# Spreading two kinds of modulation rows over partitions with TensorE in place of a trip through DRAM

## The chip, the cores and the metric

The kernel runs on one core of one Trainium2 chip. The metric is the device time of one launch in microseconds (us). Three runs of the kernel before were timed; a separate profiled execution gave the trace that is read here.

## What is computed

The reference is one step of a small hybrid backbone over 384 tokens (128 context tokens and 256 latent tokens, width 1024, all fp32), in two layers. Layer 0 mixes with a gated linear attention and a spatial gating, layer 1 with grouped-query attention. Each mixer is followed by an expert layer. What matters here:

```python
mod = silu(cond) @ w + b                    # 6 rows of 1024 for each layer and stream
h = rms_norm(x, norm_g) * (1 + scale) + shift
x = x + gate * mixer(h)                     # m[0], m[1], m[2]: shift, scale, gate of the mixer
h = rms_norm(x, norm2_g) * (1 + m[4]) + m[3]
x = x + m[5] * hier_moe(h)                  # m[5]: the gate rows of the expert layer
```

There are two streams (context and latent), so each of the six parts is a pair of rows. `hier_moe` picks two of 32 experts for each token; each expert has three matrices of 1024 x 256 floats. The rows are needed on all 128 partitions, because tokens lie on partitions and channels along them.

## The kernel before

**Weights.** All large weights pass through `ring`, six slots of 2 MB. The SP queue issues the loads in one fixed order, and before each it waits until the slot's last content is used up (`used_up`). A modulation part `(layer, part)` takes two chunks of `w_mod`, so two slots. TensorE multiplies them (`mod_products`), ScalarE copies the partial sums (`mod_part_copy`), TensorE adds them and the bias up to four rows of 512 (`mod_sum`: two halves by two streams), and ScalarE copies these four rows into the ring slot of the second chunk (`mod_row_copy`, which counts `rest_row_ready`). So the second slot stays taken until the four rows have left it. GpSimd (POOL) stores them to a DRAM tensor `mod_rows` (`store_rest`, counted in `rest_stored`), and later loads them back, read once for each of the 128 partitions (`load_rows`): a part is then 1 MB in SBUF, in `gate_rows` (GT) or `shift_scale` (GS).

**The chunks around the expert layers.** Ahead of expert layer 0 the last three parts in the ring are `norm_1` = (0, 5), the gate rows of expert layer 0, in slots 0 and 1; `router` = (1, 0), the shift rows of the attention layer's norm, in slots 2 and 3; `places` = (1, 1), its scale rows, in slots 4 and 5. Ahead of expert layer 1 the last part is `norm_3` = (1, 5), its gate rows, with its first chunk in slot 5 and its second in slot 0.

**Expert layer.** The 32 experts are taken in 16 pairs; each pair needs three loads of 2 MB (gate, up, down). Pair 0 uses slots 0 to 2, pair 1 slots 3 to 5, and so on in turn. SP issues them in the order of the slots:

```python
for u in range(2):
    for a in range(3):
        before_first(3 * u + a)
        load_experts(l, a, 2 * u, 3 * u + a)
```

so slot 0 of layer 1 waits for the last use of `norm_3`, and everything behind it in SP's order waits too. In the loop SP loads gate and up of pair q once the gate and up products of pair q-2 are done, and down of pair q once its down products are done.

**Routing and the first pairs.** The order on TensorE is: logits of three token blocks (L938), `norm_u` products and sum between them, counts (L953, L955), in layer 0 also the sum of `router` and the products of `places`, then `first_row` (L964, after `routing_sb` 3l+2), the table of all places (L968, after `routing_sb` 3l+3), in layer 0 the sum of `places`, and then the turn of the first gathered rows (L980) and pair 0 (L1008 gate and up, L1027 down). POOL gathers the token rows of a pair from `h_rows` in DRAM by an indirect DMA (L594); before the first two gathers it has stored `norm_u` (and in layer 0 `router`), and after them it stores `places` and loads the broadcast rows (L496). ScalarE copies the turned rows (L1336) and makes SiLU (L1342). VectorE works out the routing and adds the results of each pair (L1767).

Of the kernel before, what the change touches and what calls it, by code (L numbers as in the profile page):

```python
# [25 lines left out]
P = 128  # L26
D = 1024
KC = D // P
NB = 3
# [95 lines left out]
def mods(group):  # L125

    start = 0
    for name, chunks in MOD_GROUPS.items():
        if name == group:
            return range(start, start + len(chunks))  # L130
        start += len(chunks)
# [39 lines left out]
def scaled(i):  # L171

    return MODS[i][1] in (1, 4)


def fills_of(j):
# [9 lines left out]
def build(nc, d, outs):  # L186
# [3 lines left out]
    def S(name):  # L190
        if name not in sems:
            sems[name] = ctx.enter_context(nc.semaphore(name))
        return sems[name]
# [7 lines left out]
    with ctx:  # L201
# [196 lines left out]
        def used_up(eng, j):  # L398

            name, n = CHUNKS[j]  # L400
            if name == "mod" and (n < 2 * FRONT or n % 2 == 0):
                eng.wait_ge(S("mod_part_ps"), n + 1)
            elif name == "mod":
                eng.wait_ge(S("rest_stored"), 32 * (n // 2 - FRONT + 1))
            elif name == "even_in":
                eng.wait_ge(S(("qk_ps", "v_ps", "g_ps", "vg_ps", "u_ps")[n]), (4, 3, 3, 3, 4)[n])
            elif name == "even_out":
                eng.wait_ge(S("even_out_ps"), 2 * NB - 1 + n)
            elif name == "odd_in":
                eng.wait_ge(S("odd_in_ps"), (3, 6, 12)[n])  # L410
            else:
                eng.wait_ge(S("odd_out_ps"), 2 * NB - 1 + n)
# [74 lines left out]
        def _(pool):  # L487
# [3 lines left out]
            def load_rows(u, part, dst, sem):  # L491

                n = dst.shape[1]
                l = u // 2
                src = mod_rows[l, 3 * (u % 2) + part[0]:3 * (u % 2) + part[1]].rearrange("a s n -> (a s n)")
                pool.dma_start(dst, src.rearrange("(o n) -> o n", o=1).broadcast_to([P, n])).then_inc(S(sem), 16)  # L496
# [40 lines left out]
            def store_rest(group):  # L537
                for i in mods(group):
                    pool.wait_ge(S("rest_row_ready"), i - FRONT + 1)
                    _, rows, gains = rest_buffers(i)  # L540
                    if scaled(i):
                        pool.tensor_tensor(rows, rows, gains, ALU.mult).then_inc(S("gains_applied"), 1)
                        pool.wait_ge(S("gains_applied"), sum(scaled(k) for k in range(FRONT, i + 1)))
                    store_mod(i, rows, "rest_stored")
                    pool.wait_ge(S("rest_stored"), 32 * (i - FRONT + 1))

            store_rest("even")
            pool.wait_ge(S("activated"), 1)
# [17 lines left out]
            def experts(l):  # L566
                u = 2 * l + 1

                def M(name):
                    return S(f"moe{l}_{name}")  # L570

                if l == 0:
                    pool.wait_ge(S("o_ready"), NB)
                    pool.wait_ge(S("ob_ready"), NB)
                    pool.wait_ge(S("stored"), 16 * 4)
                for v in range(2):
                    pool.memset(XS[v], 0.0).then_inc(S("rows_cleared"), 1)
                pool.memset(oh_sum[:, NB, :], 0.0).then_inc(S("rows_cleared"), 1)
                store_rest(f"norm_{u}")
                if l == 0:  # L580
                    store_rest("router")

                def column(field, q):
                    return tab[:, field:field + 1, bass.ds(q, 1)]

                def one(v):
                    return v.rearrange("p (f o) -> p f o", o=1)

                def gather(q, v, static=False):
                    row = one(first_row[:, q:q + 1]) if static else column(0, q)  # L590
                    pool.tensor_copy(one(from_row[v][:, 0:1].bitcast(U32)), row).then_inc(M("row_looked_up"), 1)  # L591
                    pool.wait_ge(M("row_looked_up"), q + 1)
                    pool.sem_inc(S("pool_waited"), 1)
                    pool.indirect_dma_start(XS[v], None, h_rows[l], bass.IndirectOffsetOnAxis(ap=from_row[v][:, 0:1].bitcast(U32), axis=0),  # L594
                                            bounds_check=T - 1, oob_is_err=False).then_inc(M(f"gathered_{v}"), 16)

                def pair(q, v):
                    pool.wait_ge(M("x_ps"), q * 2 + 2)
                    pool.sem_inc(S("pool_waited"), 1)
                    gather(q + 2, v)  # L600

                pool.wait_ge(S("rows_cleared"), 3 * (l + 1))
                pool.wait_ge(S("h_stored"), 16 * NB * (l + 1))
                pool.wait_ge(S("table_ready"), 2 * l + 1)
                for q in range(2):
                    gather(q, q, static=True)
                if l == 0:
                    store_rest("places")
                load_rows(u, (2, 3), gt_t[:, :], "gate_in")
                if l == 0:  # L610
                    load_rows(2, (0, 2), gs_t[:, :], "rows_in")
                pool.wait_ge(S("table_ready"), 2 * l + 2)
                R = rounds_of(pool, l)
                with pool.Fori(0, R * (PAIRS // 2)) as i:
                    for v in range(2):
                        pair(i * 2 + v, v)
                for v in range(2):
                    pool.wait_ge(M(f"gathered_{v}"), R * 128 + 16)
                pool.sem_inc(S("pool_waited"), 1)
# [29 lines left out]
        def _(pe):  # L649
# [276 lines left out]
            def experts(l):  # L926
# [7 lines left out]
                def logits(b):  # L934
# [3 lines left out]
                        pe.matmul(to, HT[:, b, k, :], WR[:, k, :], start=(k == 0), stop=False)  # L938
                    return pe.matmul(to, ones[0:1, :], BR, start=False, stop=True)

                pe.wait_ge(S("x_updated"), 2 * NB * (u - 1) + 4)
                logits(0)
                turn_for_router(u, 1)
# [19 lines left out]
                for i in range(6):  # L963
                    mm = pe.matmul(psum[:, 5, 0:2], in_slot[:, i, :], in_first[:, i, :], start=(i == 0), stop=(i == 5))  # L964
                mm.then_inc(S("routing_ps"), 1)
                pe.wait_ge(S("routing_sb"), 3 * l + 3)
                for i in range(6):
                    mm = pe.matmul(psum[:, 7, 0:2 * PLACES], in_slot[:, i, :], in_pair[:, i], start=(i == 0), stop=(i == 5))  # L968
                mm.then_inc(S("routing_ps"), 1)
                if l == 0:  # L970
                    mod_sum(mods("places")[0])

                def turn_rows(q, v, first=False):

# [182 lines left out]
        def _(act):  # L1157
# [145 lines left out]
            def experts(l):  # L1303
# [20 lines left out]
                act.wait_ge(S("router_sub"), l + 1)  # L1324
                act.activation(g_tmp, g_tmp, ACT.Exp)
                act.activation(rival[:, :, 0:1], rival[:, :, 1:2], ACT.Exp).then_inc(S("router_exp"), 1)
                if l == 0:
                    mod_copies(mods("router"))
                    mod_copies(mods("places"))

                def x_copies(q, first=False):
                    for half in range(2):
# [86 lines left out]
        def _(dve):  # L1419
# [28 lines left out]
            def norm_apply(u, b):  # L1448

                root = rs[:, b:b + 1]  # L1450
                if u == 0:
                    dve.tensor_scalar(H[:, b, :], X[:, b, :], root, None, ALU.mult).then_inc(S("h_ready"), 2)
                    return
                dve.wait_ge(S("rows_in"), 16 * u)
                if u == 4:
                    dve.scalar_tensor_tensor(H[:, b, :], X[:, b, :], root, GS[:, 0, 0, :], ALU.mult, ALU.mult).then_inc(S("h_ready"), 1)
                    return
                s = min(b, 1)
                for n in range(2):
                    cols = slice(n * 512, (n + 1) * 512)  # L1460
                    link(dve.scalar_tensor_tensor(H[:, b, cols], X[:, b, cols], root, GS[:, 1, s, cols], ALU.mult, ALU.mult))
                    dve.tensor_tensor(H[:, b, cols], H[:, b, cols], GS[:, 0, s, cols], ALU.add).then_inc(S("h_ready"), 1)
# [5 lines left out]

            def update(u, ps, buf):

                dve.wait_ge(S("gate_in"), 16 * (u + 1))
                for c in range(6):
                    b, n = divmod(c, 2)
                    cols = slice(n * 512, (n + 1) * 512)
                    dve.wait_ge(S(ps), c + 1)
                    link(dve.tensor_tensor(buf[n], bank(OUT_BANKS[u][c]), GT[:, min(b, 1), cols], ALU.mult))
                    dve.tensor_tensor(X[:, b, cols], X[:, b, cols], buf[n], ALU.add).then_inc(S("x_updated"), 1)
                    if n == 1:
                        norm_block(u + 1, b)
                ht_low(u + 1, 2, ROUTER_TURN_BANK[u + 1] + 1)  # L1480
# [174 lines left out]
            def experts(l):  # L1655
# [166 lines left out]
                    for v in range(2):  # L1822
                        pair(i * 2 + v, v)
                dve.wait_ge(M("added"), R * (PAIRS * 6) - 6)
                dve.wait_ge(S("gate_in"), 16 * (u + 1))
                dve.wait_ge(M("x_sb"), R * (PAIRS * 2) + 2)

                def update_block(b):
# [100 lines left out]
```

## Time and profile before

| what | value |
|---|---|
| median of 3 runs | 1046.89 us (1042.3 to 1049.77) |
| profiled execution, its own time | 1044.07 us |
| its span in the trace | 1042.0 us |
| TensorE busy | 923.9 us (89%) |
| VectorE busy | 461.0 us (44%) |
| ScalarE busy | 226.1 us (22%) |
| GpSimd busy | 100.4 us (10%) |
| moved by DMA | 303.99 MB, mean 292 GB/s |
| mean granted TensorE clock | 0.953 |

The span runs from the first to the last instruction; some 2 us of the execution's own time lie around it. A busy share is an average over stages that have different limits, so what a change is worth has to be read in its stage.

### The profile page before, as it was taken

What the parts mean: (1) busy time and instruction counts of PE and PEld (TensorE: products, weight loads), DVE (VectorE), ACT (ScalarE), POOL (GpSimd) and SP (SyncE); (2) the same over time, 40 slices, a digit from 0 to 9 for tenths busy, and PEclk for the clock granted to TensorE, in tenths of its full rate; (3) what the DMA queues carried; (4) which work ended last, traced back from release to release, by engine and by line L of the source; (5) the groups of instructions that cost most, each with busy time, mean ns of one, the idle gap of its engine ahead of it and who ended that gap; (6) DMA issues with size and microseconds to landing.
All of it is one profiled execution on the core that took longest, in us unless ns stands there. A gap on an engine that the chain in (4) does not pass through costs nothing.

```text
span 1042.0 us, 11903 instructions
## 1 busy us (share of the span) xinstructions
PE 923.9 (89%) x4136; PEld 462.2 (44%) x4136; DVE 461.0 (44%) x1037; ACT 226.1 (22%) x458; POOL 100.4 (10%) x164
## 2 busy tenths in 40 slices
PE   2699999999799999999988997899589999999970
PEld 0355454645344444444433465445434444444430
DVE  1257632244323543543555474624515435435454
ACT  2223132212211112112122115212122121111121
POOL 2300011300210000000001000020100000000000
PEclk9899999998799999999998999999689999999995
DMA  9992350948899999999998523021699999999911
GB/s 301 361 351 81 132 184 18 363 167 303 341 398 419 421 420 420 419 422 420 407 372 299 178 81 131 0 87 41 259 418 419 421 420 420 421 420 420 401 50 60
DMA packets 76423, 303.99 MB, mean 292 GB/s; under 512 B 9784, under 2 KB 10096, under 8 KB 50920
## 3 DMA queue, kind: packets, MB, share of 16 engines
q1 hardware_dynamic: 66072, 277.08, 67.2%
q0 software_dynamic: 9040, 21.77, 5.9%
q10 hardware_dynamic: 1280, 4.72, 1.2%
q8 instruction: 20, 0.33, 0.1%
q14 instruction: 11, 0.09, 0.0%
HBM read 310.80 MB, written 5.32 MB: 303 GB/s over the span
## 4 chain that ended last, share of the span: by engine, by line
PE 70%; DMA 14%; DVE 7%; issue 3%; ACT 3%; SPq 2%; POOL 0%; POOLq 0%; DVEq 0%; ACTq 0%
PE psum L1008 18%; PE psum L692 16%; PE psum L1027 8%; DMA ring<-in_w_exp_up 7%; PE psum L764 4%; PE psum L890 4%; PE psum L716 3%; PE psum L980 3%; DVE ht L1767 3%; DMA arena<-h_rows,arena 3%; DMA ring<-in_w_in_odd 2%; DMA ring<-in_w_mod 2%; PE psum L938 1%; PE psum L1131 1%; PE psum L788 1%
## 5 line engine op out<-in xcount | busy, mean ns | idle before, releaser
L1008 PE MATMUL psum<-ring,arena 128*64 128x512 f32 x1024 | 229.6, 601 | 7.4 <-DMA ring<-in_w_exp_up 3.8
L692 PE MATMUL psum<-ring,ht 128*128 128x512 f32 (+1 forms) x432 | 171.9, 555 | 3.4 <-ACT ht L1199 2.7
L1008 PEld LDWEIGHTS psum<-ring,arena 128*64 128x64 f32 x1024 | 82.9, 139 | 151.3 <-issue 151.0
L1027 PE MATMUL psum<-ring,arena 128*64 128x512 f32 x512 | 116.9, 598 | 8.8 <-DVE ht L1767 7.1
L692 PEld LDWEIGHTS psum<-ring,ht 128*128 128x128 f32 x432 | 81.9, 192 | 86.2 <-issue 78.2
L1767 DVE TENSOR_TENSOR ht<-ht,psum 128x512 f32<-128x512 f32 x180 | 110.6, 681 | 4.1 <-PE psum L995 2.2
L1811 DVE TENSOR_TENSOR arena<-arena,psum 128x256 f32<-128x256 f32 x32 | 13.5, 421 | 186.0 <-ACT arena L1342 186.0
L1798 DVE SCALAR_TENSOR_TENSOR y_low<-psum,arena,y_top 128x512 fp32r<-128x512 f32 x64 | 48.0, 751 | 83.6 <-ACT y_top L1349 83.6
L1349 ACT ACTIVATE y_top<-psum,arena 128x512 fp32r<-128x512 f32 x64 | 44.0, 687 | 181.7 <-PE psum L1027 181.7
L994 PE MATMUL psum<-y_top,to_token 128*128 128x512 f32 x192 | 78.6, 409 | 3.5 <-DVE y_low L1798 3.5
L995 PE MATMUL psum<-y_low,to_token 128*128 128x512 f32 x192 | 75.6, 394 | 0.0
L716 PE MATMUL psum<-ring,cond_silu 128*32 128x512 f32 x384 | 48.0, 637 | 23.3 <-DMA ring<-in_w_mod 23.3
L1027 PEld LDWEIGHTS psum<-ring,arena 128*64 128x64 f32 x512 | 34.3, 136 | 76.6 <-issue 56.0
L1342 ACT ACTIVATE arena<-psum 128x256 f32<-128x256 f32 x32 | 12.3, 385 | 211.7 <-PE psum L1008 211.7
L980 PEld LDWEIGHTS psum<-ident,arena 128*128 128x128 f32 x272 | 34.1, 195 | 34.5 <-issue 32.1
L980 PE MATMUL psum<-ident,arena 128*128 128x128 f32 x272 | 41.0, 296 | 8.0 <-DMA arena<-h_rows,arena 8.0
L591 POOL CAST arena<-arena 128x1 uint32 (+1 forms) x36 | 7.1, 196 | 405.6 <-PE psum L980 391.2
L1336 ACT COPY arena<-psum 128x512 f32<-128x512 f32 x68 | 36.7, 589 | 31.4 <-PE psum L980 31.4
L764 PE MATMUL psum<-ht,ring 128*128 128x384 f32 x128 | 43.1, 493 | 0.0
L890 PE MATMUL psum<-ring,ht 128*128 128x512 f32 x96 | 41.9, 592 | 0.0
L994 PEld LDWEIGHTS psum<-y_top,to_token 128*128 128x128 f32 x192 | 36.2, 188 | 12.5 <-issue 5.3
L594 POOL DMA_INDIRECT arena<-h_rows,arena x36 | 37.2, 1033 | 31.2 <-POOL arena L591 30.0
(292 smaller groups left out, 869.4 us busy)
## 6 DMA issues: line engine op xcount, KB each, us to landing
ring<-in_w_exp_gate SPq DMA_DIRECT2D x32, 2048.0 KB, 18.0
ring<-in_w_exp_up SPq DMA_DIRECT2D x32, 2048.0 KB, 22.9
ring<-in_w_exp_down SPq DMA_DIRECT2D x32, 2048.0 KB, 20.5
ring<-in_w_mod SPq DMA_DIRECT2D x24, 2048.0 KB, 18.2
ring<-in_w_in_even SPq DMA_DIRECT2D x5, 2048.0 KB, 19.9
shift_scale<-mod_rows POOLq DMA_DIRECT2D x3, 2048.0 KB, 11.3
ring<-in_w_in_odd SPq DMA_DIRECT2D x3, 2048.0 KB, 21.2
ring<-in_w_out_even SPq DMA_DIRECT2D x2, 2048.0 KB, 8.5
```

The lines of the kernel that those rows point to most:

```text
L692: mm = pe.matmul(psum[:, to, 0:cols], HT[:, b, k, :], w[:, k, :], start=(k == 0), stop=(k == KC - 1))
L716: mm = pe.matmul(psum[32 * j:32 * j + 32, to, :], cond_silu[:, k, 2 - 2 * half:34 - 2 * half], w[:, k, :], start=(half == 0 and r == 0), s ...
L764: mm = pe.matmul(psum[:, to, 0:T], w[:, k, c * P:(c + 1) * P], HT[:, :, k, :], start=(k == 0), stop=(k == KC - 1))
L890: mm = pe.matmul(bank(OUT_BANKS[0][c]), HT[:, b, k, :], w[n][:, k, :], start=(k == 4), stop=(k == 3))
L980: t = pe.transpose(psum[:, half, kk * P:(kk + 1) * P], XS[v][:, 4 * half + kk:D:KC], ident[:, :])
L994: pe.matmul(to, to_token[v][:, b * P:(b + 1) * P], Y_HI[:, cols], start=True, stop=False)
L995: pe.matmul(to, to_token[v][:, b * P:(b + 1) * P], Y_LO[:, cols], start=False, stop=True).then_inc(M("back_ps"), 1)
L1008: mm = pe.matmul(psum[64 * e:64 * e + 64, 2, :], XT[:, k, 64 * e:64 * e + 64], RG[:, 3 * v:3 * v + 2, e, k, :], start=(k == 0), stop=(k == ...
L1027: mm = pe.matmul(psum[64 * e:64 * e + 64, 4 + n, :], HTS[v][:, k, 64 * e:64 * e + 64], RD[:, 3 * v + 2, e, k, n * 512:(n + 1) * 512], star ...
L1349: act.activation(Y_HI[:, n * 512:(n + 1) * 512], bank(4 + n), ACT.Copy, scale=token[v][:, 1:2]).then_inc(M("y_top"), 1)
L1767: dve.tensor_tensor(acc, acc, found, ALU.add).then_inc(M("added"), 1)
L1798: dve.scalar_tensor_tensor(Y_LO[:, cols], bank(4 + n), token[v][:, 1:2], Y_HI[:, cols], ALU.mult, ALU.subtract).then_inc(M("y_low"), 1)
```

## The change

Two parts of layer 0's tail, `norm_1` and `router`, and `norm_3` ahead of expert layer 1, no longer go through DRAM. TensorE multiplies the four rows by a one-hot matrix (one column of the identity's first four rows, repeated over 128 columns), which puts one of the four rows on all 128 partitions of a PSUM bank; four such products make a part. ScalarE copies each bank into GT or GS. Three banks are used in turn, so the fourth and later products wait for a copy. The ring slot is free once the four products are done (`spread_ps`), not once a store has landed. `places` keeps its path through DRAM. On TensorE the products stand between L964 and L968, and in layer 0 the sum of `places` is moved ahead of them.

```diff
+SPREAD = [mods(name)[0] for name in ("norm_1", "router", "norm_3")]
+SPREAD_BANKS = {0: (0, 1, 4), 1: (2, 3, 0)}
+
+def stores_until(i):
+    return 32 * sum(k not in SPREAD for k in range(FRONT, i + 1))
...
             elif name == "mod":
-                eng.wait_ge(S("rest_stored"), 32 * (n // 2 - FRONT + 1))
+                if n // 2 in SPREAD:
+                    eng.wait_ge(S("spread_ps"), 4 * SPREAD.index(n // 2) + 4)
+                else:
+                    eng.wait_ge(S("rest_stored"), stores_until(n // 2))
...
-                store_rest(f"norm_{u}")
-                if l == 0:
-                    store_rest("router")
...
-                load_rows(u, (2, 3), gt_t[:, :], "gate_in")
                 if l == 0:
-                    load_rows(2, (0, 2), gs_t[:, :], "rows_in")
+                    load_rows(2, (1, 2), gs_t[:, 2 * D:4 * D], "rows_in")
...
+                def spread(i, done):
+                    pe.wait_ge(S("rest_row_ready"), i - FRONT + 1)
+                    for c in range(4):
+                        if done + c >= 3:
+                            pe.wait_ge(S("rows_spread"), 8 * l + done + c - 2)
+                        pe.matmul(bank(SPREAD_BANKS[l][(done + c) % 3]), ident[0:4, c:c + 1].broadcast_to([4, P]), rest_buffers(i)[1],
+                                  start=True, stop=True).then_inc(S("spread_ps"), 1)
...
                 mm.then_inc(S("routing_ps"), 1)
+                if l == 0:
+                    mod_sum(mods("places")[0])
+                    spread(mods("norm_1")[0], 0)
+                    spread(mods("router")[0], 4)
+                else:
+                    spread(mods("norm_3")[0], 0)
                 pe.wait_ge(S("routing_sb"), 3 * l + 3)
                 for i in range(6):
                     mm = pe.matmul(psum[:, 7, 0:2 * PLACES], in_slot[:, i, :], in_pair[:, i], start=(i == 0), stop=(i == 5))
                 mm.then_inc(S("routing_ps"), 1)
-                if l == 0:
-                    mod_sum(mods("places")[0])
+                pe.wait_ge(S("rows_spread"), (8, 12)[l])
...
+                def spread_copies(rows, done):
+                    for c in range(4):
+                        half, s = divmod(c, 2)
+                        act.wait_ge(S("spread_ps"), 8 * l + done + c + 1)
+                        act.copy(rows[:, s, half * 512:(half + 1) * 512], bank(SPREAD_BANKS[l][(done + c) % 3])).then_inc(S("rows_spread"), 1)
+
                 if l == 0:
                     mod_copies(mods("router"))
                     mod_copies(mods("places"))
+                act.wait_ge(S("x_updated"), 2 * NB * u)
+                spread_copies(GT, 0)
+                if l == 0:
+                    act.wait_ge(S("h_ready"), 2 * NB * (u + 1))
+                    spread_copies(GS[:, 0], 4)
...
-                dve.wait_ge(S("gate_in"), 16 * (u + 1))
+                dve.wait_ge(S("rows_spread"), (8, 12)[l])
```

VectorE also waits for `rows_spread` ahead of the attention layer's norm, and the counts of `gate_in` follow the loads that are left.

## Rows read from the trace of the kernel before

**Rows 1.** The page's strip of 40 slices, its row of GB/s.

```profile
GB/s 301 361 351 81 132 184 18 363 167 303 341 398 419 421 420 420 419 422 420 407 372 299 178 81 131 0 87 41 259 418 419 421 420 420 421 420 420 401 50 60
```

**Rows 2.** The page's DMA issues: size of one, median us to landing.

```profile
ring<-in_w_exp_up SPq DMA_DIRECT2D x32, 2048.0 KB, 22.9
...
shift_scale<-mod_rows POOLq DMA_DIRECT2D x3, 2048.0 KB, 11.3
...
gate_rows<-mod_rows POOLq DMA_DIRECT2D x4, 1024.0 KB, 9.5
```

**Rows 3.** Windows of expert layer 0: clock, DMA share and GB/s stand last.

```profile
261.00:263.00 2.00, 2.00 (x20) 0.73 (x13) 0.00 (x0) 0.34 (x1) 0.00 (x0) 1.00 0.50 74
263.00:284.00 21.00, 14.98 (x77) 8.64 (x76) 9.20 (x39) 3.53 (x7) 5.90 (x9) 0.78 0.99 401
284.00:288.00 4.00, 3.60 (x10) 1.28 (x12) 0.00 (x0) 1.40 (x2) 1.12 (x2) 0.50 0.43 117
...
361.00:517.00 156.00, 151.04 (x706) 71.58 (x706) 68.77 (x150) 28.67 (x51) 11.94 (x20) 1.00 1.01 420
```

**Rows 4.** Windows of expert layer 1, same columns.

```profile
733.00:740.60 7.60, 4.99 (x15) 2.53 (x14) 4.65 (x29) 2.17 (x4) 1.04 (x2) 0.50 0.13 19
...
835.00:986.00 151.00, 145.62 (x681) 69.34 (x680) 65.31 (x145) 27.66 (x49) 11.29 (x20) 1.00 1.01 420
```

**Rows 5.** The chain that ended last: start us, us, what.

```profile
361.35 7.10 PE psum L1008 x32
...
369.19 23.01 DMA ring<-in_w_exp_up
392.54 7.09 PE psum L1008 x32
...
921.87 22.84 DMA ring<-in_w_exp_up
945.05 7.09 PE psum L1008 x32
...
991.24 6.87 PE psum L1008 x32
```

**Rows 6.** SP's queue in time order: when the first expert loads are issued.

```profile
261.17 0.37 SPq L425 DMA_DIRECT2D ring<-in_w_exp_up  x1
...
739.14 0.37 SPq L425 DMA_DIRECT2D ring<-in_w_exp_gate  x1
```

**Rows 7.** Timeline of routing and the first turn in layer 0.

```profile
268.36 1.50 PE L964 MATMUL psum<-arena 128*128 128x2 f32 x12
...
273.10 4.37 PE L968 MATMUL psum<-arena 128*128 128x200 f32 x12 [3.24 <-DVE arena L1744]
...
277.91 1.05 PE L733 MATMUL psum<-ring,pick 128*4 128x512 f32 x2
...
279.32 0.58 ACT L1184 COPY ring<-psum 4x512 f32<-4x512 f32 x1 [10.24 <-PE psum L734]
...
281.55 1.94 PE L980 MATMUL psum<-ident,arena 128*128 128x128 f32 x8 [2.27 <-DMA arena<-h_rows,arena]
...
284.40 8.98 PE L1008 MATMUL psum<-ring,arena 128*64 128x512 f32 x32 [0.91 <-ACT arena L1336]
```

**Rows 8.** Timeline of routing in layer 1.

```profile
733.72 1.87 PE L733 MATMUL psum<-ring,pick 128*4 128x512 f32 x2
...
743.26 2.72 PE L964 MATMUL psum<-arena 128*128 128x2 f32 x12 [3.10 <-DVE arena L1726]
...
749.22 3.88 PE L968 MATMUL psum<-arena 128*128 128x200 f32 x12 [3.24 <-DVE arena L1744]
```

**Rows 9.** Timeline of layer 1's first turn and pair 0.

```profile
757.21 1.94 PE L980 MATMUL psum<-ident,arena 128*128 128x128 f32 x8 [4.11 <-DMA arena<-h_rows,arena]
...
759.92 8.45 PE L1008 MATMUL psum<-ring,arena 128*64 128x512 f32 x32 [0.77 <-ACT arena L1336]
```

**Rows 10.** TensorE's waits from 361 to 517 us: total, times, longest.

```profile
PE psum L1008 <- DMA ring<-in_w_exp_up: 1.3, 4, 0.3
```

More of the change, by code:

```diff
@@ L544, in store_rest @@
                     store_mod(i, rows, "rest_stored")
-                    pool.wait_ge(S("rest_stored"), 32 * (i - FRONT + 1))
+                    pool.wait_ge(S("rest_stored"), stores_until(i))
             store_rest("even")
@@ L1454, in norm_apply @@
                 dve.wait_ge(S("rows_in"), 16 * u)
+                if u == 2:
+                    dve.wait_ge(S("rows_spread"), 8)
                 if u == 4:
@@ L1469, in update @@
             def update(u, ps, buf):
-                dve.wait_ge(S("gate_in"), 16 * (u + 1))
+                dve.wait_ge(S("gate_in"), 16 * (u // 2 + 1))
                 for c in range(6):
@@ L1824, in experts @@
                 dve.wait_ge(M("added"), R * (PAIRS * 6) - 6)
-                dve.wait_ge(S("gate_in"), 16 * (u + 1))
+                dve.wait_ge(S("rows_spread"), (8, 12)[l])
                 dve.wait_ge(M("x_sb"), R * (PAIRS * 2) + 2)
```

## The prediction

> **What bounds the kernel now.** I read the page's strip of slices first. It shows two long plateaus in which DMA moves 420 GB/s and is busy all the time [rows 1]: the two expert layers, in which nearly all bytes are expert weights. The second view, windows, makes it sharp: over 361 to 517 us and over 835 to 986 us the 16 DMA engines have a share of 1.01 and move 420 GB/s without a break [rows 3, 4]. TensorE is at 96 to 97% in the same windows, so it is not obvious which of the two sets the pace. The chain of waits tells: in layer 0 it passes through the load of an up matrix of 23.01 us just ahead of the gate and up products at 392.54 us, and in layer 1 through one of 22.84 us ahead of those at 945.05 us [rows 5]. TensorE's waits there look tiny, 1.3 us in all [rows 10]. That is how two nearly equal rates look: the bytes of a pair are 3 x 2.10 MB (2048 KB each, rows 2) and a gather, which takes at least 15.0 us at 420 GB/s, and the pairs come every (392.54 - 361.35) / 2 = 15.6 us. So what counts in an expert layer is when its stream of weights starts, what else is in that stream, and its rate. The end follows, as the wait at 945.05 us is only 46 us from the last pair's products at 991.24 us [rows 5].
>
> The third view is SP's queue. The second expert load of layer 0 is issued at 261.17 us, and the first of layer 1 at 739.14 us [rows 6]. In both cases SP was waiting for the store of a modulation part to land, `norm_1` and `norm_3`. Just before, DMA is nearly idle: 74 GB/s over 261 to 263 us, 19 GB/s over 733 to 740.6 us [rows 3, 4].
>
> **The change, part by part.**
>
> *Bytes removed.* In layer 0 the broadcast of the gate rows (1024 KB = 1.05 MB) goes, and of the broadcast into `shift_scale` (2048 KB) half goes; in layer 1 the gate rows go [rows 2]. All three were moved while DMA was the bound. At 420 GB/s each 1.05 MB is 2.5 us, so -5.0 us in layer 0 and -2.5 us in layer 1. The small stores (4 KB) are worth nothing in bytes. For memory transfers to SBUF the Trainium skill ("SBUF — State Buffer", its guidance on end-to-end transfer time) advises to reckon with about 358 GB/s, bound by HBM; the trace contradicts it here with 420 GB/s, and by the page's figure the three removals would come to 8.8 us, not 7.5, and the sum below would be some 1 us lower.
>
> *The release of slot 0 in layer 1.* Now this slot waits for the fourth product of the spread of `norm_3` (`spread_ps` 12), and these stand on TensorE behind L964. L964 waits for VectorE's routing until 743.26 us and takes 2.72 us, so it ends at 745.98 us [rows 8]. The trace has no product with four rows as input and 128 columns of weights; the nearest are L733 (128 rows, 4 columns, 512 moving): two in 1.87 us at half clock, that is 0.94 us each [rows 8], and two in 1.05 us at full clock, 0.52 us each [rows 7]. TensorE is at a granted clock of 0.50 in this stretch [rows 4], so I take 4 x 0.9 = 3.6 us with 2.1 us as the lower end. The fourth also waits for ScalarE's first copy. The trace's copies of 512 PSUM columns take 0.58 us [rows 7], and this one starts about 0.9 us after 745.98 us, so it is done before the third product is and costs nothing; ScalarE has nothing queued there, and if its first copy were late, each us of it would go onto the loads. So `spread_ps` 12 comes at 748.1 to 749.6 us, I take 749.3 us. SP issues the load then rather than at 739.14 us: 10.2 us later (9.0 to 10.6). Behind this load stand all six first loads in SP's order, as slot 0 is first.
>
> Of these 10.2 us the removed gate rows give 2.5 us back. The first gather (some 48 rows of 4 KB, 0.2 MB by 768 assignments over 16 pairs) now moves while DMA is idle: 0.5 us. Net: **+7.2 us** on every load of layer 1 (6.0 to 8.0).
>
> *Does it reach the end?* Pair 0 starts at 759.92 us now, because the turn of its rows waited 4.11 us for a gather that shared DMA with the weights [rows 9]. That wait goes: the gather is issued as before, on an idle DMA. L968 starts at 749.5 us in place of 749.22 us, as the spread fills TensorE's wait of 3.24 us [rows 8]. But what is late next is the weights: issued at 749.3 us, data from about 1.5 us later (SP issues at 739.14 us, and the window's idle part ends at 740.6 us, rows 4, 6), 4.2 MB for gate and up take 10 us, so pair 0 starts at 761.5 to 762.5 us, 2 us later. The later pairs follow the weights, as the plateau is the bound: they are 7 us later, and so is the end.
>
> *The releases in layer 0.* Slot 0 is free as before. Slot 1 now waits for `spread_ps` 4. On TensorE, L964 ends at 269.86 us; then the moved sum of `places`. It takes 1.9 us now, from the end of L968 at 277.47 us to the copy at 279.32 us, so it ends at about 271.9 us. Its inputs are there, and it is hidden in the wait for VectorE, which ends at 273.10 us. The products of `norm_1` follow. ScalarE first copies the two results of `places`, 0.58 us each [rows 7], so its first spread copy starts at 273.1 us and ends at 273.7 us; the fourth product waits for it and ends at 274.3 us. From there on the pace is ScalarE's copy, 0.55 us: the eighth product ends at 276.5 us (`spread_ps` 8, slot 3). L968 is queued behind the eighth product and starts at 276.5 us in place of 273.10 us; VectorE's table waits for it, as does the turn for pair 0. L968 then ends at 280.9 us at most, and the turn, which waited 2.27 us for its gather until 281.55 us [rows 7], is not later. Slot 1, issued at 274.4 us, has landed by 281 to 282 us, so pair 0 starts at about 284 us, as now (284.40 us, rows 7). POOL loses two stores in front of the first gathers and is a little earlier; nobody needs it.
>
> The weights of slots 1 and 2, issued at 261.17 us and behind it, move 13.2 us later, and slots 3 and 4 some 4 us later. In bytes: over 263 to 284 us DMA moved 401 GB/s and over 261 to 263 us 74 GB/s, 8.6 MB, plus 0.5 MB up to 288 us [rows 3]; the new stream starts at 276.0 us and moves 5.2 MB by 288.4 us, where the old one is back at the full rate. One gather of 0.25 MB goes into the idle stretch. So 9.1 - 5.4 = 3.7 MB are missing, 8.7 us; the two removed broadcasts give back 2.1 MB, 5.0 us. That leaves 3.7 us; with the second gather in the idle stretch too it would be 3.1 us. I take **+3.3 us** (1.5 to 4.5). The layer is bound by the stream from 392 us at the latest, so these 3.3 us reach its end, and the loads for the attention layer behind it.
>
> *The rest.* VectorE's waits for `rows_spread` are met hundreds of us before they are asked. 12 products and 12 copies are 6 to 11 us of TensorE and 7 us of ScalarE, in stretches in which both waited; their cover is VectorE's routing, and without it they would cost the 3 us by which the spread of layer 0 outlasts it.
>
> **Sum.** 7.2 + 3.3 = 10.5 us on the profiled execution's own 1044.07 us gives 1054.6 us. This execution lies 2.8 us under the median of 1046.89 us and inside the runs' spread, so the median after should lie between 1054.6 and 1057.4 us; I give 1055.
>
> **The rivals.**
>
> *The cushion absorbs it (not slower).* If TensorE and not DMA sets the pace of the pairs, a late start of the stream is caught up. The six slots let loads run ahead by two pairs, and TensorE's busy 96% and its waits of 1.3 us speak for it [rows 3, 10]. It decides if a pair takes TensorE 15.6 us even with weights at hand. Then layer 1 pays only pair 0's 2 us and layer 0 nothing: 1046 us. The unbroken 420 GB/s and the chain through 23 us loads speak against it. Chance 0.25 with the cases in which half is absorbed.
>
> *The bytes win (faster).* If the first products after L964 came early and pair 0 were not held, the removed 7.5 us would remain: about 1037 us. Against it stands SP's order, which puts the first load behind L964 in any case. Chance 0.04.
>
> *The start costs more.* TensorE idles in layer 1 from about 756 to 762 us and pair 0 then runs at half clock (8.45 us at a clock partly 0.5 now, 13 us at worst by twice 6.87 us, rows 5, 9); gate and up of pair 2 are issued late and the stream breaks for 2 to 4 us; or in layer 0 the copies and products run one after the other, 8 x 0.5 us more. 1058 to 1061 us. The queue holds six loads of 5 us each at that time, which speaks against a break. Chance 0.16.
>
> The forecast has 0.55. The range of 8 in 10 takes in its bounds (7.5 to 12.5 us), the spread of the runs and the near part of both neighbours: 1047 to 1062 us. About 1% (10.5 us) is what a measurement of this kernel can tell from no change. The forecast lies right at that border, so its chance is split almost evenly; with the rivals: faster 0.04, same 0.50, slower 0.46.
>
> **What the profile after would show.** The first expert load of layer 1 issued at 748 to 750 us plus layer 0's shift, behind four products of 0.5 to 0.9 us; DMA near zero from 733 us until then; pair 0's products released by DMA and not by ScalarE; L1008 of the last pair 10.5 us later than 991.24 us; DMA's share at 1.01 in both plateaus. In layer 0, a gap without traffic from 261 to 276 us. The forecast is wrong if the plateaus show DMA under 1.00 (TensorE is the bound), if pair 5 or so of a layer is no later than now, or if the loads leave within 5 us of their old place.

## The result, and the profile after

The kernel after took 1060.62 us in the median of four runs (1057.52 to 1063.9), the kernel before 1047.17 us. The ratio is 1.0134, with a 95% interval of 1.008 to 1.0189, so it is 1.3% slower. Six later runs of the same kernel gave 1.016 (1.013 to 1.0191). The profiled execution took 1057.87 us, its span is 1055.8 us, 13.8 us more than before.

The strip of slices of the page after, its row of GB/s, answers to [rows 1]. Both plateaus are there at 420 GB/s; what has changed most is ahead of them (slice 11 with 197 in place of 341, and slices 27 to 29 with 10, 60 and 123 in place of 87, 41 and 259).

```profile
GB/s 307 362 331 80 126 189 16 368 155 299 197 421 419 420 421 420 419 421 420 406 379 327 123 122 88 76 10 60 123 421 419 421 419 420 421 420 420 410 61 60
```

The windows of layer 0 and layer 1 after, with granted clock, DMA share and GB/s last, answer to [rows 3, 4]:

```profile
263.00:277.00 14.00, 14.00 (x68) 5.74 (x68) 7.13 (x29) 4.45 (x8) 3.61 (x5) 0.87 0.07 19
277.00:279.00 2.00, 2.00 (x4) 0.91 (x3) 0.00 (x0) 0.67 (x2) 1.71 (x3) 0.50 0.81 168
279.00:284.00 5.00, 5.00 (x7) 1.46 (x5) 0.00 (x0) 1.69 (x4) 0.06 (x1) 0.50 0.96 383
...
361.00:523.00 162.00, 156.98 (x730) 74.39 (x730) 73.43 (x158) 29.01 (x51) 12.93 (x21) 1.00 1.01 420
```

```profile
752.00:757.00 5.00, 5.00 (x7) 1.60 (x6) 1.39 (x6) 1.69 (x4) 2.90 (x3) 0.50 0.18 45
...
849.00:1000.00 151.00, 145.47 (x680) 73.41 (x679) 64.83 (x144) 27.64 (x49) 11.23 (x20) 1.00 1.01 420
```

Where DMA moved 401 GB/s over 263 to 284 us before, it now rests until 277 us. The plateaus have kept their rate and their share of 1.01.

The timeline of the kernel after, of layer 0 and then of layer 1, answers to [rows 6 to 9]. L981 is the `first_row` of before's L964, L955 the spread, L1354 its copy, L991 before's L968, L1030 before's L1008, and the L437 rows are SP's first loads.

```profile
268.59 1.50 PE L981 MATMUL psum<-arena 128*128 128x2 f32 x12
...
271.61 12.34 PE L955 MATMUL psum<-ring,ident 4*128 4x512 f32 x16
...
277.14 0.37 SPq L437 DMA_DIRECT2D ring<-in_w_exp_up  x1
```

```profile
746.94 2.72 PE L981 MATMUL psum<-arena 128*128 128x2 f32 x12 [3.10 <-DVE arena L1762]
...
749.59 7.19 PE L955 MATMUL psum<-ring,ident 4*128 4x512 f32 x8
...
755.11 0.58 ACT L1354 COPY gate_rows<-psum 128x512 f32<-128x512 f32 x1 [1.12 <-PE psum L955]
756.71 4.37 PE L991 MATMUL psum<-arena 128*128 128x200 f32 x12
756.81 0.37 SPq L437 DMA_DIRECT2D ring<-in_w_exp_gate  x1
...
770.18 5.22 PE L1030 MATMUL psum<-ring,arena 128*64 128x512 f32 x12 [7.99 <-DMA ring<-in_w_exp_up]
```

The reader is to see three things. SP's first load of layer 1 leaves less than 0.1 us after the four products end (756.81 and 749.59 + 7.19 us). The later copies wait 1.07 to 1.12 us each for a product, and not the products for the copies. And pair 0 is released by its weights after 8 us of waiting, where before the gathered rows were the last to come.

The end of the chain after, against [rows 5]:

```profile
757.22 12.87 DMA ring<-in_w_exp_up
770.18 9.51 PE psum L1030 x32
...
1005.67 6.87 PE psum L1030 x32
```

**Where the time went.** Runs of one kernel differ by some us in stretches that the change doesn't touch, so I compare spans between two points inside an expert layer: from the start of `first_row` (L964, and the line that holds it in each other kernel) to the start of the last pair's gate and up products. In layer 1 this is 991.24 - 743.26 = 247.98 us before [rows 5, 8] and 1005.67 - 746.94 = 258.73 us after, 10.7 us more. In layer 0 it is 516.63 - 268.36 = 248.27 us before (the chain of waits has the last pair at 516.63 us) and 523.03 - 268.59 = 254.44 us after, 6.2 us more. That makes 16.9 us. The stretch from layer 0's last pair to layer 1's `first_row` was 2.7 us shorter (226.63 and 223.91 us), which the change doesn't explain.

### The profile page after: what moved, and what is told of

Its sections match the earlier page's. It is cut to its first block, busy times and chain, and to the rows that moved or that the text cites. A ratio compares the mean times of both kernels' runs of the same rounds, so it can differ in the third digit from the quotient of the medians.

```text
span 1055.8 us, 11956 instructions
## 1 busy us (share of the span) xinstructions
PE 940.1 (89%) x4160; PEld 475.4 (45%) x4160; DVE 460.6 (44%) x1037; ACT 232.7 (22%) x470; POOL 96.6 (9%) x156
## 4 chain that ended last, share of the span: by engine, by line
PE 67%; DMA 18%; DVE 5%; issue 3%; ACT 3%; SPq 2%; DVEq 0%; POOL 0%; ACTq 0%
PE psum L1030 18%; PE psum L700 16%; DMA ring<-in_w_exp_up 15%; PE psum L1049 7%; PE psum L772 4%; PE psum L898 4%; PE psum L724 3%; DVE ht L1803 2%; PE psum L1002 2%; DMA ring<-in_w_in_odd 2%; DMA ring<-in_w_mod 2%; PE psum L955 2%; PE psum L946 1%; PE psum L1153 1%; PE psum L796 1%
## 5 line engine op out<-in xcount | busy, mean ns | idle before, releaser
L1030 PE MATMUL psum<-ring,arena 128*64 128x512 f32 x1024 | 229.7, 599 | 20.6 <-DMA ring<-in_w_exp_up 15.8
L1030 PEld LDWEIGHTS psum<-ring,arena 128*64 128x64 f32 x1024 | 90.3, 138 | 157.8 <-issue 148.9
L1049 PEld LDWEIGHTS psum<-ring,arena 128*64 128x64 f32 x512 | 34.3, 136 | 76.6 <-issue 56.0
```

Of the source, the lines that this page charges most:

```text
L1030: mm = pe.matmul(psum[64 * e:64 * e + 64, 2, :], XT[:, k, 64 * e:64 * e + 64], RG[:, 3 * v:3 * v + 2, e, k, :], start=(k == 0), stop=(k == ...
L1049: mm = pe.matmul(psum[64 * e:64 * e + 64, 4 + n, :], HTS[v][:, k, 64 * e:64 * e + 64], RD[:, 3 * v + 2, e, k, n * 512:(n + 1) * 512], star ...
```

## The experiments

All times of stretches below are between the same two points, in us:

| kernel | layer 0 | layer 1 | ratio to before (95%) |
|---|---|---|---|
| before | 248.27 | 247.98 | |
| after | 254.44 | 258.73 | 1.0134 (1.008 to 1.0189) |
| layer 1 undone | 254.85 | 247.87 | 1.0061 (1.0014 to 1.0107) |
| after, slots released at the sum | 245.37 | 242.65 | 0.988 (0.9842 to 0.9917) |
| before, late first load in layer 1 | 249.10 | 254.73 | 1.0064 (1.0034 to 1.0093) |
| before, without gate bytes in layer 1 | 249.47 | 245.41 | 0.9979 (0.9945 to 1.0013) |
| after, norm_3 products in fp32r | 254.81 | 254.60 | 1.0095 (1.0064 to 1.0125) |
| after, products of 128 rows | 252.96 | 258.12 | 1.0111 (1.0077 to 1.0145) |
| slots released, shift spread moved back | 242.54 | 242.78 | 0.9854 (0.9826 to 0.9881) |
| before, slots released at the sum | 246.16 | 244.94 | 0.9922 (0.9894 to 0.9949) |
| after once more | 253.19 | 258.45 | 1.016 (1.013 to 1.0191) |

Layer 0 was the same code in three of these kernels (before, late first load, without gate bytes) and gave 248.27 to 249.47; after's layer 0 stood in four (after twice, layer 1 undone, norm_3 in fp32r) and gave 253.19 to 254.85. So layer 0 owes 5.4 us by the means (248.9 and 254.3), known to about 1 us. Layer 1 repeats within 0.3 us and owes 10.7 us.

**Undo the change in layer 1 alone.**

```diff
-SPREAD = [mods(name)[0] for name in ("norm_1", "router", "norm_3")]
+SPREAD = [mods(name)[0] for name in ("norm_1", "router")]
...
+                if l == 1:
+                    store_rest("norm_3")
...
+                else:
+                    load_rows(3, (2, 3), gt_t[:, :], "gate_in")
...
-                else:
-                    spread(mods("norm_3")[0], 0)
```

> Kernel after, with the gate rows of expert layer 1 (norm_3) sent through DRAM again and layer 0 left as changed. Theory (the weight stream's start and bytes decide): in the two traces the last pair of layer 1 is 14.4 us late, and L964 of layer 1 was 3.7 us late already, so layer 1 owes 10.7 us; this kernel should lie 10 to 11 us under the kernel after and 3 to 4 us over the kernel before, with the first load of layer 1 issued 4.1 us before its L964, as before the change. Rival (the extra products and copies of TensorE and ScalarE cost the time, wherever they stand): 4 of 12 products go, so a third, some 5 us under the kernel after.

Measured: 1052.77 us, ratio 1.0061. In the timeline the first load leaves 4.1 us before `first_row`, as in the kernel before:

```profile
749.88 0.37 SPq L437 DMA_DIRECT2D ring<-in_w_exp_gate  x1
...
754.01 2.72 PE L985 MATMUL psum<-arena 128*128 128x2 f32 x12 [3.10 <-DVE arena L1765]
```

Layer 1 is back at 247.87 us. By the ratios the run is 0.7% (8 us) under the first runs of the kernel after and 1.0% (10 us) under the later ones, where I expected 10 to 11 us. It is 6 us over the kernel before, not 3 to 4: I had taken layer 0's share from how late layer 1's `first_row` was, and that includes the stretch between the layers, which varies. The stretches give layer 0's share as 5 to 6 us, which fits. This run alone doesn't tell work from waiting, as it takes both away.

**Release the slots at the sum, keep all products in place.**

```diff
+            if i in SPREAD:
+                rows = (HID_ROWS, HTS_ROWS, HID_ROWS)[SPREAD.index(i)]
+                return RC[:, slot, 0, :], rows, None
...
-                    eng.wait_ge(S("spread_ps"), 4 * SPREAD.index(n // 2) + 4)
+                    eng.wait_ge(S("mod_sum_ps"), n // 2 - FRONT + 1)
```

> Kernel after, with the four rows of the three spread parts written not into the ring but into the hidden-layer buffers that are free at that time, and SP released at the sum (mod_sum_ps). All products and copies stay where they are, so TensorE's work is the same. Theory: layer 1's first load leaves some 10 us before L964 ends (3 us earlier than in the kernel before), the stream is ahead and pair 0 starts as TensorE allows, near its place before; 1040 to 1050 us, so 10 us or more under the kernel after. Rival (TensorE's extra work is the cost): no change from the kernel after, 1058 to 1062 us.

Measured: 1034.35 us, ratio 0.988, so 26 us under the kernel after with the same products and copies, and under the expected 1040 to 1050 us.

```profile
734.47 0.37 SPq L442 DMA_DIRECT2D ring<-in_w_exp_gate  x1
...
741.60 2.72 PE L986 MATMUL psum<-arena 128*128 128x2 f32 x12 [3.10 <-DVE arena L1767]
744.25 7.19 PE L960 MATMUL psum<-arena,ident 4*128 4x512 f32 x8
...
758.19 7.09 PE L1035 MATMUL psum<-ring,arena 128*64 128x512 f32 x32 [0.81 <-ACT arena L1375]
```

The four products still take 7.19 us in front of pair 0, and pair 0 starts 16.6 us after `first_row`, as before the change (759.92 - 743.26 us, rows 8, 9). So this place costs TensorE nothing in layer 1. What cost the time was that SP waited for it. It was more than I expected; the last kernels below divide it. The rival, that the extra work is the cost, is out for the kernel after. In layer 0 the work isn't free once the slots are released early: pair 0 starts 20.9 us after `first_row` there, where it was 16.0 us before the change, and the kernel with the shift spread moved back shows what that is worth.

**The kernel before with a late first load and nothing else.**

```diff
+            sp.wait_ge(S("routing_ps"), 7)
             experts(1, lambda slot: used_up(sp, last_in(slot, len(CHUNKS))))
```

> Kernel before, with one wait more: SP issues the loads of expert layer 1 only after L964 of that layer (routing_ps 7). Nothing else is changed. Theory: the loads leave 7 us later (746 us in place of 739), everything in layer 1 after them too, so the run is 6 to 7 us longer. Rival (the six slots are a cushion, TensorE is the bound): 0 to 2 us longer, as pair 0 alone waits.

Measured: 1052.29 us, ratio 1.0064.

```profile
748.27 2.72 PE L965 MATMUL psum<-arena 128*128 128x2 f32 x12 [3.10 <-DVE arena L1727]
...
751.03 0.37 SPq L425 DMA_DIRECT2D ring<-in_w_exp_gate  x1
...
1003.00 6.87 PE psum L1009 x32
```

The first load leaves 2.76 us after `first_row` and not 4.12 us before it: 6.9 us later. The last pair is 6.75 us later (254.73 against 247.98). Within the scatter of 0.3 us all of the delay reaches the end; the six slots absorb none of it.

**The kernel before without 1 MB.** This kernel leaves out the broadcast of the gate rows in layer 1, so that layer 1's expert update uses other gate rows.

```diff
-                load_rows(u, (2, 3), gt_t[:, :], "gate_in")
                 if l == 0:
+                    load_rows(u, (2, 3), gt_t[:, :], "gate_in")
```

> Kernel before, which leaves out the 1 MB broadcast of the gate rows in expert layer 1 (the update at the end then multiplies by the attention layer's gate rows, so the output isn't the reference's). Theory: DMA is the bound, 1.05 MB at 420 GB/s are 2.5 us: 2 to 3 us shorter. Rival (TensorE is the bound): no change.

Measured: ratio 0.9979, with an interval that holds 1, so the runs alone show nothing. In the trace layer 1 is 2.6 us shorter (986.72 - 741.31 = 245.41 us), as 1.05 MB at 420 GB/s should be, against a scatter of 0.3 us.

**Cheaper products for norm_3.** The gate rows of layer 1 are rounded in this kernel from fp32 to fp32r, the type in which the kernel already keeps `y_top` and `y_low`.

```diff
+                        one_hot, rows = (pick_bias[0:4, 2 * c:2 * c + 1], ROWS_3) if l else (ident[0:4, c:c + 1], rest_buffers(i)[1])
-                        pe.matmul(bank(...), ident[0:4, c:c + 1].broadcast_to([4, P]), rest_buffers(i)[1], ...
+                        pe.matmul(bank(...), one_hot.broadcast_to([4, P]), rows, ...
```

> Kernel after; the rows and the one-hot of norm_3 are in fp32r, so that a product is one record and not two (the gate rows of layer 1 are rounded by it). Theory (the four products stand in front of SP's first load, each us of them goes onto the end): a product falls from 1.71 us to 0.6 to 0.9 us, the first load of layer 1 leaves 3 to 4.4 us earlier after the end of L964's products, and the last pair follows by as much, so 3 to 4.5 us under the kernel after. Rival (the products fill a wait of TensorE and cost nothing): no change from the kernel after.

Measured: 1058.12 us, ratio 1.0095. The timeline has four records where there were eight:

```profile
755.52 2.72 PE L985 MATMUL psum<-arena 128*128 128x2 f32 x12 [3.10 <-DVE arena L1766]
...
760.51 0.37 SPq L440 DMA_DIRECT2D ring<-in_w_exp_gate  x1
```

```profile
758.17 2.31 PE L959 MATMUL psum<-rows,pick_bias 4*128 4x512 f32 x4
```

The first load leaves 4.99 us after the start of `first_row`, where it was 9.87 us: 4.9 us earlier. Layer 1 is 4.1 us shorter, against a scatter of 0.3 us. So the price of the products is on the path, though not quite one for one. The runs alone don't separate this kernel from the first runs of the kernel after (1.0064 to 1.0125 against 1.008 to 1.0189); the stretch does.

**Products of 128 rows.**

```diff
-                        pe.matmul(bank(...), ident[0:4, c:c + 1].broadcast_to([4, P]), rest_buffers(i)[1],
+                        pe.matmul(bank(...), ident[:, c:c + 1].broadcast_to([P, P]), RC[:, slot_of(CHUNKS.index(("mod", 2 * i + 1))), 1, :],
```

> Kernel after; the one-hot has all 128 rows and so has the moving operand (the rows below the fourth are multiplied by zero), for all 12 products. It asks whether the half clock under the products, 1.71 us each, comes with their four rows. If so, the granted clock stays at or returns to 1.00 in layer 0's stretch, a product takes 1.0 us there, slot 1 and slot 3 are released 2 and 5 us earlier, and the run is 2 to 6 us shorter than the kernel after. If the clock falls for another reason (a share of idle time before them), the products stay at 1.7 us and the time stays.

Measured: 1060.43 us, ratio 1.0111, so not told apart from the kernel after. What it says of the clock stands in the last section. A product in layer 0 fell from 1.5 us (12.34 / 8) to 0.89 us (7.13 / 8):

```profile
274.99 7.13 PE L955 MATMUL psum<-ring,ident 128*128 128x512 f32 x16
...
278.72 0.37 SPq L437 DMA_DIRECT2D ring<-in_w_exp_up  x1
```

The first release (slot 1) came 6.8 us after `first_row` and not 8.6 us, 1.8 us earlier, and layer 0 is 1.5 us shorter than in the first trace of after, which is little more than the scatter of 1 us there. The release of slot 3 came 5.2 us earlier and added nothing that can be seen; the loads of slots 1 and 2, 2 MB each, had 10 us of transfer in front of it. In layer 1 the four products fell from 7.19 to 6.12 us, the first load left 1.1 us earlier, and the layer is 0.6 us shorter. I had expected 2 to 6 us in all; the stretches give 2.1 us. It is the start of the stream that counts, and not the release behind it.

**Release early, and move the shift rows' spread behind the expert layer.**

```diff
                 if l == 0:
                     mod_sum(mods("places")[0])
                     spread(mods("norm_1")[0], 0)
-                    spread(mods("router")[0], 4)
...
+                if l == 0:
+                    spread_shift()
                 combine(R * PAIRS - 1, 1)
```

> As the kernel with slots released at the sum, with the rows kept in free columns of the arena and the four products and copies of router (the shift rows of the attention layer) moved behind the loop of expert layer 0, where TensorE then waits for odd_in. Theory (with the slots released early TensorE sets layer 0's pace, as all its gate and up products start 15.1 us apart): the four products no longer stand ahead of pair 0, which starts some 5 us earlier after L964, and layer 0 is 4 to 5 us shorter; behind the loop they are hidden by the load of odd_in. 1028 to 1032 us. Rival (the stream is the bound after all, or the four products are on the path behind the loop): 1033 to 1037 us, as with the slots alone.

Measured: 1033.74 us, ratio 0.9854, in the range of the rival (1033 to 1037 us) and not in that of the theory. Pair 0 starts 15.4 us after `first_row` and not 20.9 us, 5.5 us earlier, but the last pair of layer 0 is only 2.8 us earlier. The chain of waits shows why: the gate and up products have 6.87 us and a distance of 15.1 us up to the pair at 422.45 us, and from the one at 468.15 us on 7.09 us and 15.4 us. I read this as TensorE setting the pace first, and then the stream. So each of the two theories holds for a part of the layer. Against the kernel with the slots alone (0.988, 0.9842 to 0.9917) the runs can't tell it apart; against the kernel before it is 1.5% faster (0.9826 to 0.9881), the lowest ratio here.

```profile
422.45 6.87 PE psum L1041 x32
...
468.15 7.09 PE psum L1041 x32
...
514.34 6.87 PE psum L1041 x32
```

**The kernel before with the slots released early.** All rows go through DRAM as before; only their source is outside the ring.

```diff
+            if i in OUTSIDE:
+                return RC[:, slot, 0, :], (ROWS_A, ROWS_B, ROWS_A)[OUTSIDE.index(i)], None
...
+                if n // 2 in OUTSIDE:
+                    eng.wait_ge(S("mod_sum_ps"), n // 2 - FRONT + 1)
```

> Kernel before (all rows through DRAM), with the four rows of norm_1, router and norm_3 kept in free columns of the arena and SP released at the sum. It asks what of the gain over the kernel before belongs to the early release and what to the removed broadcasts. If the start of the stream alone decides, layer 1 is 3 us shorter (first load 3 us earlier against L964, the 1 MB broadcast stays), layer 0 1 to 2 us shorter, in all 1042 to 1044 us. If the removed bytes are worth nothing, it is as fast as the kernel with the shift spread moved back, 0.985 of the kernel before.

Measured: 1038.42 us, ratio 0.9922 (0.9894 to 0.9949). That is between the two cases: under the 1042 to 1044 us of the start alone, and over 0.985.

```profile
731.12 0.37 SPq L434 DMA_DIRECT2D ring<-in_w_exp_gate  x1
...
738.25 2.72 PE L973 MATMUL psum<-arena 128*128 128x2 f32 x12 [3.10 <-DVE arena L1735]
```

The first load leaves 7.1 us before `first_row` and not 4.1 us, and layer 1 is 3.0 us shorter (244.94). Layer 0 is 2 to 3 us shorter than in the three kernels with before's layer 0. The two stretches together give 5 to 6 us and the runs 8 us; the rest isn't explained. So about half of the gain of the best version is the early release alone, and the other half comes with the spread in TensorE, once it no longer holds the slots: in layer 1 that is 2.2 us (244.94 and 242.78), near the 2.5 us of the removed gate rows, and in layer 0 3.6 us (246.16 and 242.54).

**The kernel after again.**

> The kernel after once more, on the chip of the run before it, for its distance to the kernel before and for the spread of the stretch between the two expert layers, which differed by 2.7 us between the first two traces. The sum of the two expert layers, taken from first_row to the last pair in each, should again be 16 to 18 us longer than before.

Measured: 1063.87 us, ratio 1.016 (1.013 to 1.0191). Against the stretches of the first trace before, the two layers are 4.9 and 10.5 us longer, 15.4 us in all, a little less than I expected. The first load of layer 1 leaves 9.87 us after `first_row`, as in the first trace. The stretch between the layers is 227.85 us here and was 223.91 us in the first trace of the same kernel, so that difference belongs to the run and not to the change. In the kernels with before's layer 0 it is 224.85 to 228.27 us.

## Why the prediction was right, and where it was too small

The direction, the place and the mechanism held: SP's first loads wait for the spread, and the stream of weights carries the delay to the end. The size was too small. The time of 1060.6 us lies near the upper end of the range of 1047 to 1062 us, above the stated 1055 us and above the 1054.6 to 1057.4 us of the sum. Of the three cases it was *slower by over 1%*, which I gave 0.46, less than the 0.50 for the case within 1%. That the range held is in part luck: it had been widened toward the rival *the start costs more*, in whose band of 1058 to 1061 us the time lies, and that rival had the wrong reason.

*The bound.* Right. Both plateaus keep 420 GB/s, and the late first load shows that 6.9 us of a later start are 6.75 us at the end. The cushion (0.25) is refuted for layer 1 as it was before. It exists in another state: in the kernel with the shift spread moved back, where the stream starts early, TensorE sets the pace for some ten pairs, and then the lead of the stream is used up. The prediction named a DMA share under 1.00 as the sign that TensorE is the bound. That sign doesn't work: in that kernel the share is 1.01 and the rate 420 GB/s over 361 to 452 us too. The distance of the pairs tells, 15.1 us there and 15.6 us in the kernel before.

*Bytes removed.* Right in layer 1: 2.6 us for 1.05 MB, where I had 2.5 us. For layer 0 no run takes its two broadcasts away alone; they are shown only together with the rest.

*The release of slot 0 in layer 1.* This is the step that failed in size. I took a product of the spread as 0.9 us, from L733 with "x2" and 1.87 us, which I read as two products [rows 8]. But `mod_sum` issues one product there: a product of fp32 is two records in the trace. The same rows had it: L964 and L968 are loops over six products and stand there as x12 [rows 7, 8]. The right reading was 1.87 us for one. Measured: eight records, 7.19 us for four products, not 3.6 us. The first load leaves 9.87 us after the start of `first_row`, and the prediction had 6.0 us (749.3 - 743.26). The 3.8 us of difference, a little reduced, are the step from the forecast 7.2 us to the measured 10.7 us. The fp32r products confirm it: 2.31 us for the four, 4.1 us back.

*The releases in layer 0.* The same error. `spread_ps` 4 was forecast 6.0 us after the start of `first_row` and slot 1 was loaded 8.6 us after it. I also took the pace of the later products from ScalarE's copy of 0.55 us; in fact ScalarE waited 1.07 to 1.18 us for each product from the third on, so the products were the pace, at half clock. 3.3 us forecast, 5.4 us measured, known to 1 us. With the 2.6 us by which slot 1 was loaded later than forecast, the working comes out at 5.9 us. All twelve products took 12.34 + 7.19 = 19.5 us of TensorE, where I had 6 to 11 us.

*The start costs more* (0.16). Its place was right, its mechanism wasn't: pair 0 did run slowly (9.51 us) after a wait of 8 us, but the stream never broke, with 419 to 423 GB/s from 759 us on.

*The sum* of measured terms is 5.4 + 10.7 = 16.1 us, against 10.5 us. The two measured ratios, 1.0134 and 1.016, are 14 and 17 us.

## What to carry to other kernels

When a buffer of a ring is given back by a later step, the price of a change to this step is not its own duration but how much later the first load behind it leaves; look at what the loads' queue waits for first, and if the step uses only a small part of the buffer, copy this part out and release at once. Read a duration of a new product from a row of which the count per instruction is known: check "xN" against the code, as one line of code can be several records. And where two engines are nearly equal, work moved from one to the other pays only as long as the first is the bound: take from the stream what comes free, and then look again at who sets the pace.

## What the runs showed of the hardware

The granted clock fell to half under products of four rows although TensorE was busy all the time. The same window of two kernels, the one with four rows (after) and the one with 128 rows, in which only the products differ:

```profile
263.00:284.00 21.00, 21.00 (x76) 8.11 (x75) 7.13 (x29) 6.82 (x13) 5.38 (x7) 0.75 0.35 120
```

```profile
263.00:284.00 21.00, 21.00 (x116) 9.60 (x109) 8.20 (x36) 8.30 (x16) 5.40 (x7) 0.98 0.26 89
```

Busy is 21.00 of 21.00 us in both. The products start at 271.61 us with four rows and at 274.99 us with 128, and from 265 us up to there the clock was 1.00 (the level of 2.4 GHz) in both. Over the window it is 0.75 with four rows, and 0.50 (the level of 1.2 GHz) in each window from 277 to 284 us, nearly all of it under the products, but 0.98 with 128 rows. So a product with four rows took 1.5 us in the mean of layer 0 (12.34 us for eight) and 1.8 us in layer 1 (7.19 us for four), and the same product with 124 rows of zeros in its one-hot took 0.89 us in layer 0. In layer 1 both kinds start at 0.50. Four rows left the clock there to the end of the products; under the 128 rows it rose to a mean of 0.86 over 758 to 760 us, before they ended at 759.78 us.

The kernel with the shift spread moved back has a third case. Its four products of four rows stand behind the expert loop of layer 0, after a long stretch at full clock:

```profile
529.26 3.81 PE L958 MATMUL psum<-arena,ident 4*128 4x512 f32 x8
```

The clock is 1.00 over 529 to 532 us and 0.50 over 533 to 536 us, with the engine busy all the time, and the 128-row products behind them take 0.63 us each where they took 0.40 us ahead of them. The kernel with the slots released alone has no such products there and keeps 1.00 from 525 to 538 us.

The Trainium skill ("TensorE: Matmul & The Clock Gate", Part 1) lets the clock go by how busy the engine has been; here the busy time was the same, so the busy time of the trace isn't what decides. That the number of rows is the cause is shown by the one pair of kernels in which it alone differs; how many rows are enough wasn't tried.

In fp32r the same product is one record, 0.58 us at the same place at which the fp32 product takes two records and 1.8 us.
